# The down projection of a feed-forward layer: seven half-size products in place of eight, with weight sums added by DMAs

## The reference, cut to what matters

```python
h = rms_norm(x, norm_ffn[l])                                         # 512 x 1024
x = x + (jax.nn.silu(h @ w_gate[l]) * (h @ w_up[l])) @ w_down[l]     # (512 x 2816) @ (2816 x 1024)
return x
```

## Time and profile before

| what | us |
|---|---|
| median of three runs | 1574.59 (1573.61 to 1575.96) |
| the profiled execution: span | 1570.6 |
| TensorE busy | 1536.9 (98%) |
| VectorE busy | 1007.2 (64%) |
| ScalarE busy | 832.5 (53%) |
| GpSimd busy | 210.5 (13%) |

### The profile page before, as it was taken

One profiled execution on the slowest core, in us unless ns is written; L12 is line 12 of the kernel. 1 busy time (PEld: TensorE's weight loads), 2 busy tenths in 40 slices (PEclk: granted clock), 3 DMA queues, 4 the chain that ended last, 5 costly groups with the idle time before them and its releaser, 6 DMA issues.

```text
span 1570.6 us, 20022 instructions
## 1 busy us (share of the span) xinstructions
PE 1536.9 (98%) x7872; PEld 1247.3 (79%) x7872; DVE 1007.2 (64%) x1681; ACT 832.5 (53%) x1459; POOL 210.5 (13%) x278
## 2 busy tenths in 40 slices
PE   9999999999999999999989999999999999999999
PEld 8877777788877888888877766888778888888887
DVE  4267977865479998999787786575765333434231
ACT  5278776554456888888863434435434333333220
POOL 1000014522234000000062101111201000000000
PEclk9999999999999999999999999999999999999999
DMA  6122121114547999999943111031212323223232
GB/s 233 65 81 79 56 71 65 54 54 150 214 161 231 375 421 421 421 422 421 326 149 107 54 54 54 28 108 54 81 58 78 108 81 108 92 82 121 67 112 90
DMA packets 78641, 235.89 MB, mean 150 GB/s; under 512 B 6960, under 2 KB 9424, under 8 KB 66256
## 3 DMA queue, kind: packets, MB, share of 16 engines
q1 hardware_dynamic: 68288, 207.62, 36.3%
q10 hardware_dynamic: 6624, 14.88, 2.5%
q0 software_dynamic: 3632, 12.08, 2.0%
HBM read 221.97 MB, written 12.60 MB: 149 GB/s over the span
## 4 chain that ended last, share of the span: by engine, by line
PE 84%; DVE 11%; ACT 2%; issue 1%; DMA 1%; POOL 0%; SPq 0%; DVEq 0%; ACTq 0%; POOLq 0%
PE bank L109 80%; PE bank L112 4%; DVE low L134 2%; DVE REST L124 1%; DVE REST L134 1%; DVE REST L137 1%; ACT REST L115 1%; DVE AL L124 1%; DVE REST L146 1%; DVE REST L143 1%; DVE REST L130 1%; ACT REST L118 1%; ACT CHH L118 0%; DVE R L124 0%; DVE st L140 0%
## 5 line engine op out<-in xcount | busy, mean ns | idle before, releaser
L124 DVE TENSOR_TENSOR low<-slot,CHH 128x1024 fp32r<-128x1024 f32 (+1 forms) x300 | 298.0, 1037 | 117.5 <-ACT CHH L118 116.5
L118 ACT ACTIVATE CHH<-slot 128x1024 fp32r<-128x1024 f32 (+1 forms) x300 | 258.8, 900 | 128.7 <-PE bank L109 56.6
L134 DVE SCALAR_TENSOR_TENSOR low<-slot,smalls,CHH 128x512 fp32r<-128x512 f32 (+1 forms) x232 | 170.3, 766 | 191.2 <-ACT CHH L118 187.3
L109 PE MATMUL bank<-AH,CHH 128*128 128x512 f32 (+1 forms) x640 | 248.5, 388 | 0.2 <-DVE AL L124 0.2
L109 PE MATMUL bank<-AL,CHH 128*128 128x512 f32 (+1 forms) x640 | 242.8, 379 | 0.0
L109 PE MATMUL bank<-AH,low 128*128 128x512 f32 (+1 forms) x640 | 242.6, 379 | 0.0
L118 ACT ACTIVATE CHH<-slot,smalls 128x512 fp32r<-128x512 f32 (+1 forms) x232 | 154.6, 701 | 137.8 <-PE bank L109 68.2
L109 PE MATMUL bank<-CHH,AH 128*128 128x512 f32 x512 | 215.2, 420 | 3.8 <-DVE low L134 2.8
L109 PE MATMUL bank<-low,AH 128*128 128x512 f32 x512 | 200.8, 392 | 0.0
L109 PE MATMUL bank<-CHH,AL 128*128 128x512 f32 x512 | 200.2, 391 | 0.0
L109 PE MATMUL bank<-CHH,XTF 128*128 128x512 f32 x512 | 161.2, 396 | 1.9 <-DVE REST L121 1.1
(11 more groups left out here) (191 smaller groups left out, 2395.4 us busy)
## 6 DMA issues: line engine op xcount, KB each, us to landing
slot<-in_w_in SPq DMA_DIRECT2D x35, 1024.0 KB, 5.1
slot<-in_w_exp_gate SPq DMA_DIRECT2D x32, 1024.0 KB, 13.0
slot<-in_w_exp_up SPq DMA_DIRECT2D x32, 1024.0 KB, 13.2
slot<-in_w_exp_down SPq DMA_DIRECT2D x32, 1024.0 KB, 13.2
slot<-in_w_gate SPq DMA_DIRECT2D x10, 1024.0 KB, 4.9
slot<-in_w_up SPq DMA_DIRECT2D x10, 1024.0 KB, 5.0
slot<-in_w_down SPq DMA_DIRECT2D x10, 1024.0 KB, 5.1
slot<-in_w_out SPq DMA_DIRECT2D x8, 1024.0 KB, 5.1
```

What stands on the lines that cost most here:

```text
L109: return self.e.matmul(out, l, r, start=start, stop=stop) if self.e else Issued()
L118: return self.e.activation(out, in_, ACT.Copy, scale=scale) if self.e else Issued()
L124: return self.e.tensor_tensor(out, a, b, op) if self.e else Issued()
L134: return self.e.scalar_tensor_tensor(out=out, in0=a, scalar=s, in1=b, op0=op0, op1=op1) if self.e else Issued()
```

## The change

Rows of hidden features, tokens and output columns are each halved, and Strassen's scheme in Winograd's form is used: seven products of half size (256 tokens x 1408 features x 512 columns) in place of eight. A product has 11 chunks, and a chunk has 6 matmuls (two token tiles x 3) in place of 12. With A the activations and B the weights, P1 = A11 B11, P2 = A12 B21, P3 = S4 B22, P4 = A22 T4, P5 = S1 T1, P6 = S2 T2, P7 = S3 T3.

- Activations: `up_evac` writes the product into `parts`; GpSimd forms S3 for the first eleven feature blocks and S1, S2, S4 for the others, each 128x256, S2 after S1 and S4 after S2. High parts and low parts of A12, S2, S3, A22, S1 and S4 are made during the down projection, in pieces of up to three blocks (128x768), low parts in place.
- Weights: P1 and P2 load their chunks as before, though splits now take two chunks at once (128x1024; the eleventh chunk alone). P6, P7 and P4 run together over eleven "triples". A triple is one slot with B11, B12, B21 of one feature block, loaded by two DMAs (512 KB and 256 KB), then GpSimd issues a DMA that adds B22 onto B12 in the slot, then VectorE makes two more sums (`weight_sums`), and the three chunks are split at once (128x1536). Triples use five slots, two of them in memory that comes free at the end of `fu20` and of P1. For P5 three slots get B11 (1 MB, 1 MB, 768 KB) and a DMA each that adds B12. P3 loads B22 plainly.
- Order on TensorE: P1, P2, the triples, P5, P3. VectorE's and ScalarE's work is listed unit by unit (a unit `u` is one split: 0 to 5 for P1, 6 to 11 for P2, 12 to 22 the triples, 23 to 28 P5, 29 to 34 P3). P6 and P5 are summed on top of P1 in its banks, after VectorE has added the former sum onto `xr`.

The core of the diff:

```diff
+    def dma_add(self, out, in_):
+        return self.e.dma_start(out, in_, accum_op=ALU.add) if self.e else Issued()
...
-    slot_kb = (0, 8, 16, 48, 144, 152, 160, 136, 176)
+    slot_kb = (0, 8, 16, 48, 144, 152, 160, 136, 176, 94, 104)
...
-    for n in range(2):
-        plan_seg(f"wd{n}", t["w_down_2"][0], 512 * n, 0, nk=FT, part=3)
+    down_rows = t["w_down_2"][0].rearrange("(t k p) n -> p t k n", t=2, p=P)
+    def unit(s, q0, n, at, ready):
+        u = len(units)
+        chunks = range(len(CH), len(CH) + n)
+        for i, c in enumerate(chunks):
+            CH.append((s, q0 + i))
+        cells = range(at, at + n)
+        before = [holds_cell[x] for x in cells if x in holds_cell]
+        holds_cell.update((x, chunks[-1]) for x in cells)
+        units.append((chunks, s.ap[:, q0:q0 + n, :], s.low[:, q0:q0 + n, :],
+                      of[:, a:a + n * 512].rearrange("p (k n) -> p k n", k=n), before, ready))
+    holds_cell = {(D0 - 1 - x) % 8: D0 - 1 - x for x in range(8)}
+    pair_cells = itertools.cycle((0, 2, 4, 6))
+    def plan_block(h, n0, add_row=None):
+        for k in range(0, FK, 4):
+            m = min(4, FK - k)
+            s = plan_slot(next(in_turn), down_rows[:, h, k:k + m, n0:n0 + 512], m, 512, 3)
+            if add_row is not None:
+                s.more = down_rows[:, h, k:k + m, add_row:add_row + 512]
+            for q in range(0, m, 2):
+                unit(s, q, min(2, m - q), next(pair_cells), ("added", s.number) if s.more is not None else None)
+    plan_block(0, 0)
+    plan_block(1, 0)
+    in_turn = itertools.cycle((9, 10, next(in_turn), next(in_turn), next(in_turn)))
+    triples = []
+    for j in range(FK):
+        s = plan_slot(next(in_turn), down_rows[:, 0, j, :].rearrange("p (b n) -> p b n", b=2), 3, 512, 3)
+        s.rest = down_rows[:, 1, j, 0:512]
+        s.more = down_rows[:, 1, j, 512:1024]
+        taken[s.i] += 1
+        s.landed += 16
+        triples.append(s)
+        unit(s, 0, 3, 3 * (j % 2), ("T4", j))
+    pair_cells = itertools.cycle((6, 8, 3, 0))
+    plan_block(0, 0, add_row=512)
+    sums_last = [s for s in slots if s.more is not None][FK:]
+    plan_block(1, 512)
...
+        def product(name, c, part, k, two, first, last):
+            hi, lo = high(c), low(c)
+            pe.wait_ge(*at(("part", part, k if part == A11 else k // 3)))
+            pe.wait_ge(*at(("", "lo", c)))
...
+        sums = pair("P1")
+        for k in range(FK):
+            product("P1", D0 + k, A11, k, sums, k == 0, k == FK - 1)
+        own2 = pair("P2")
+        for k in range(FK):
+            product("P2", D0 + FK + k, A12, k, own2, k == 0, k == FK - 1)
+        own7, own4 = pair("P7"), pair("P4")
+        for i in range(2):
+            pe.wait_ge(*at(("on x", "P1", i, 0)))
+        for k in range(FK):
+            c = D0 + 2 * FK + 3 * k
+            product("P6", c, S2, k, sums, False, k == FK - 1)
+            product("P7", c + 1, S3, k, own7, k == 0, k == FK - 1)
+            product("P4", c + 2, A22, k, own4, k == 0, k == FK - 1)
+        for i in range(2):
+            pe.wait_ge(*at(("on x", "P6", 2 + i, 0)))
+        for k in range(FK):
+            product("P5", D0 + 5 * FK + k, S1, k, sums, False, k == FK - 1)
+        banks.next["main"] += 2
+        own3 = pair("P3")
+        for k in range(FK):
+            product("P3", D0 + 6 * FK + k, S4, k, own3, k == 0, k == FK - 1)
...
+        def unit_high(chunks, raws, lows, highs, before, ready):
+            act.wait_ge(*at(ready) if ready else landed(chunks[0]))
+            for c in before:
+                act.wait_ge(*at(("", "done", c)))
+            act.copy(highs, raws).then_inc(*mark("act_hi", *(("", "hi", c) for c in chunks)))
...
+        def high_of(part, n, *events):
+            for event in events:
+                act.wait_ge(*at(event))
+            act.copy(piece(part_high[part], n), piece(parts[:, part], n), scale=-1.0 if part == S1 else 1.0).then_inc(
+                *mark("act_evac", ("part high", part, n)))
+        gates_done = ("full", "fu20", 1)
...
+            if 15 <= u <= 18:
+                high_of(S1, u - 15, ("", "done", D0 + 2 * FK - 1))
+            if 19 <= u <= 22:
+                high_of(S4, u - 19, ("", "done", D0 + 2 * FK - 1))
...
+        def first_low(k):
+            dve.wait_ge(*at(("S2", k)))
+            dve.wait_ge(*at(("part high", A11, k)))
+            dve.tt(parts_low[:, A11, k, :], parts[:, A11, k, :], part_high[A11][:, k, :].bitcast(F32), ALU.subtract).then_inc(
+                *mark("dve_evac", ("part", A11, k)))
+        def unit_low(chunks, raws, lows, highs, before, ready):
+            for c in chunks:
+                dve.wait_ge(*at(("", "hi", c)))
+            dve.tt(lows, raws, highs.bitcast(F32), ALU.subtract).then_inc(*mark("dve_lo", *(("", "lo", c) for c in chunks)))
         for f0 in range(0, FT, 4):
             def up_evac(j, f0=f0):
                 f = f0 + j
-                s = sgp.buf(("sg", f))
+                of = A11 if f < FK else A12
                 dve.wait_ge(*at(("full", f"fu{f0}", j)))
                 dve.wait_ge(*at(("fgs", f)))
-                dve.tt(s, s, banks.ap((f"fu{f0}", j)), ALU.mult).then_inc(
-                    *mark("dve_evac", ("fum", f), ("free", (f"fu{f0}", j))))
-                dve.wait_ge(*at(("aTh", f)))
-                dve.tt(aT[1][:, f, :], s, aT[0][:, f, :].bitcast(F32), ALU.subtract).then_inc(
-                    *mark("dve_evac", ("aT", f), ("free", ("sg", f))))
+                dve.tt(parts[:, of:of + 2, f % FK, :], *(x.rearrange("p (t n) -> p t n", t=2) for x in (
+                    sgp.buf(("sg", f)), banks.ap((f"fu{f0}", j)))), ALU.mult).then_inc(
+                    *mark("dve_evac", ("a", f), ("free", (f"fu{f0}", j)), ("free", ("sg", f))))
+                if FK + 2 <= f < FT - 1:
+                    first_low(f - FK - 2)
             if f0:
                 drain(seg(f"fg{f0}"))
-            drain(seg(f"fu{f0}", up_evac))
-        for n in range(2):
-            def out_x(i, n=n):
-                xs = xr[:, i, n * 512:(n + 1) * 512]
-                dve.wait_ge(*at(("full", f"wd{n}", i)))
-                dve.wait_ge(*at(("x4", i, n)))
-                dve.tt(xs, banks.ap((f"wd{n}", i)), xs, ALU.add).then_inc(
-                    *mark("dve_evac", ("out", i, n), ("free", (f"wd{n}", i))))
-            drain(seg(f"wd{n}", out_x))
+            for n, _ in enumerate(seg(f"fu{f0}", up_evac)):
+                if f0 == 20 and n in EARLY_UNITS:
+                    unit_low(*units[EARLY_UNITS.index(n)])
+        def low_of(part, n):
+            dve.wait_ge(*at(("part high", part, n)))
+            dve.wait_ge(*at(("S4", FK - 1)))
+            a, b, c = piece(parts_low[:, part], n), piece(parts[:, part], n), piece(part_high[part], n).bitcast(F32)
+            x = dve.stt(a, b, -1.0, c, ALU.mult, ALU.subtract) if part == S1 else dve.tt(a, b, c, ALU.subtract)
+            x.then_inc(*mark("dve_evac", ("part", part, n)))
+        def weight_sums(j):
+            b11, b12, b21 = (triples[j].ap[:, q, :] for q in range(3))
+            dve.wait_ge(*at(("added", triples[j].number)))
+            dve.tt(b11, b12, b11, ALU.add).then_inc(*mark("dve_down", ("T2", j)))
+            dve.wait_ge(*at(("T2", j)))
+            dve.tt(b21, b11, b21, ALU.add).then_inc(*mark("dve_down", ("T4", j)))
+        last_on = {(i, n): ("x4", i, n) for i in range(NT) for n in range(2)}
+        def add_on(name, half, n, bank=None, left=False, done=False):
+            for i in range(2):
+                to = 2 * half + i, n
+                xs = xr[:, to[0], n * 512:(n + 1) * 512]
+                dve.wait_ge(*at(("full", name, i)))
+                dve.wait_ge(*at(last_on[to]))
+                last_on[to] = ("on x", name, *to)
+                events = [last_on[to]]
+                if left:
+                    events.append(("free", (name, i)))
+                if done:
+                    events.append(("out", *to))
+                b = banks.ap((bank or name, i))
+                dve.tt(xs, *((xs, b, ALU.subtract) if n and name != "P3" else (b, xs, ALU.add))).then_inc(*mark("dve_evac", *events))
+        for u, unit in enumerate(units):
+            if 11 <= u < 11 + FK:
+                weight_sums(u - 11)
+            if u >= len(EARLY_UNITS):
+                unit_low(*unit)
+            if u == 1:
+                first_low(FK - 3)
+            if u == 2:
+                first_low(FK - 2)
+                first_low(FK - 1)
+            if 3 <= u <= 4:
+                for n in (2 * u - 6, 2 * u - 5):
+                    low_of(A12, n)
+            if 5 <= u <= 6:
+                for n in (2 * u - 10, 2 * u - 9):
+                    low_of(S2, n)
+            if 7 <= u <= 8:
+                for n in (2 * u - 14, 2 * u - 13):
+                    low_of(S3, n)
+            if u == 9:
+                add_on("P1", 0, 0)
+            if 10 <= u <= 11:
+                for n in (2 * u - 20, 2 * u - 19):
```

(48 more changed lines are left out.)

## The result

The changed kernel takes 1585.64 us (median of four runs, 1584.45 to 1589.07) against 1574.30 for the kernel before: ratio 1.0075, interval 1.0062 to 1.0088. It is 0.75% slower, where 1572.0 was forecast and 1582 was the upper end of the range.

The account below looks back on a forecast made before the run. TensorE alone was taken to bound the down projection. 15.0 us removed, less losses of 5.7 + 2.0 + 4.6 = 12.3, leaves 2.7 gained: 1567.9 profiled, runs 4.0 above, written as 1572.0; range 1565 to 1582.

Parts of the forecast that it names:

- 15.0 us removed: Down projection on TensorE: seven products need 462 matmuls instead of 528, so 66 at 0.2273 us go.
- First loss: From T to the first triple: VectorE's list delays its start to T+35.7 instead of T+30.0, 5.7 us lost.
- T: Zero point of the down projection's times: end of `fu20`, 1447.4 us in the kernel before.
- VectorE's account: VectorE's work before the first triple: free at T+7.2, then 27.7 us of list, plus 0.5 and 0.3, giving T+35.7.
- Second loss: In the triples: how fast a slot comes round through load, addition, sums and split; triples end at T+82.8, 2.0 us lost.
- the rule: Triples' slots: four triples need 4.7 + L + 1.4 + 1.7 + 4.1 us, more than TensorE's 16.4 once L exceeds 4.5.
- L: Time of GpSimd's adding DMA for a triple's slot, taken from gathers: 5.5 us, bounds 4.4 and 8.8.
- Third loss: Way into P5: P6's sum stands behind unit 25, which awaits a 1 MB addition; P5 starts at T+87.4, 4.6 us lost.
- The clock, a rival: Gaps before the first triple and P5 lower TensorE's clock, 18 matmuls costing 4 us more each time: 1576 to 1580; chance 0.10.
- The queues' latency counts, not their rate: Down projection's DMAs: 26 MB in 117 us is 222 GB/s, where 421 was sustained in the experts' stretch.
- The slow rival: Adding DMAs slow, L = 8.8 and 12 us for 1 MB; triples end at T+90.8, kernel at 1579.4; chance 0.18.

Follow-up runs that it names:

- the late pieces: Changed kernel with P3 ahead of P5, plus nine of the S2, S3, A22 pieces split during the triples and P3 instead of before: ratio 1.0021, span 1578.5.

## Why the prediction was wrong, step by step

- **15.0 us removed:** right; where TensorE has no gap it needs 0.229 us a matmul.
- **First loss, 5.7 forecast, 5.9 measured:** the first triple starts at 1483.81 = T+35.9 against T+35.7. VectorE's account held to 0.2 us, the wait of 2.9 us included. That the first triple's own load and addition held it to nearly the same place (T+35.2 with the late pieces) was not in it; only that run showed it.
- **Second loss, 2.0 forecast, 9.6 measured (the triples end at T+90.5).** The way of a slot is what bound the triples: without its additions they need 42.1 us between the low parts, and with six slots and earlier issues 41.2. The terms of the rule (11.9 + L for four triples, 17.4 us by the forecast) were mis-sized: one round of the chain, from 1502.02 to 1522.97, takes 21.0 us. L was put at 5.5 and is 0.3 + 5.0 in the median, but 0.3 + 7.5 in the chain; the load was put at 4.7 and is 0.3 + 5.3 in the median, 0.3 + 5.2 in the chain. So the median of L was forecast well; the round that counted was not the median one. I had taken the additions' own price from a gather, right for one alone, and not asked what they do to the loads beside them: they hold an engine 2.4 times as long as a copy. 1.6 of the 9.6 us is the clock behind the first wait (eight matmuls 0.2 us late each).
- **Third loss, 4.6 forecast, 9.2 measured.** The mechanism and the place were right (unit 25, the second 1 MB addition, the sum P6 behind it). The addition was put at 9.2, which is near what one takes alone (8.9 to 10.5), and took 14.2, beside P5's first addition for 7 us of it (with six slots, issued after the first had landed, it took 11.4); that these DMAs overlap was not in the estimate. Its load was put at 5.1 and took 6.5; the slot came free at T+75.1 instead of T+69.5. The wait is what of this sticks out behind the triples.
- **The clock, a rival with a chance of 0.10:** it came true at both gaps, 1.6 us and 32.3 - 30.0 = 2.3 us, less than its price of 4 us each (its 18 matmuls come from no row; eight were slow behind the first gap). It was no alternative to the other losses but their consequence. The forecast itself had a gap of 4.6 us ahead of P5, and every wait that long lowered the clock in these runs, so that cost belonged in the sum; the one ahead of the first triple, of about 3 us, lowered it in four of the six runs in which it was 2.9 us long.
- **"The queues' latency counts, not their rate":** half right for the triples, whose loss ended without quicker additions once the way of a slot had more room, and wrong for P5, where the engines' share is 1.09 while its additions are in flight together. In the earlier trace rows the down projection takes a share of 0.26 for 90 GB/s, so by this estimate its loads would fill the engines at about 346 GB/s, not 422; its packets are of 2 KB, the experts' of 6.4 KB in the mean (80.93 MB in 12715), which I take for the reason without having tried it. An addition then takes 2.4 times a copy's engine time. The row with the share was in the table and I didn't divide; the 2.4 was in no row.

The slow rival named the right mechanism, with L = 8.8 and 12 us, and gave 1579.4. With the clock's 3.9 us it would be 1583. Its T+90.8 for the end of the triples against T+90.5 is luck in part: L was less than 8.8, the first triple did not wait for its own addition, and the clock added its share. The sum of the measured losses is 5.9 + 9.6 + 9.2 + 2.3 = 27.0, less 15.0: 12.0 of the 12.7 us; T is 0.4 us later and the end behind the last matmul 0.2 us longer.

## What to carry to other kernels

When work moves from a full engine to idle ones, add up the way of one buffer (release, load, addition, sums, split, use) and divide by the buffers, with each DMA at its price beside the others; divide a stretch's GB/s by its DMA share to see roughly what the engines would carry there. A wait of TensorE of 3.3 us or more needs the clock's 1.8 to 3.2 us beside it in the sum; one of 2.1 to 2.9 us cost it here in seven cases of fourteen. A gain can lie in the queue rather than in the data: one addition moved up one unit was worth 5.9 us, and P3 ahead of P5, late pieces, one more slot and earlier loads together made this change faster than the kernel before (0.9944).

## What was not expected of the hardware

An adding DMA held the engines 2.4 times as long as a copy of the same bytes, and plain 256 KB loads beside it landed after 5.3 us instead of 4.1. Two 1 MB additions in flight together took 11.0 and 14.2 us where one alone took 8.9 to 10.5. TensorE's granted clock fell after some idle waits of 2.1 to 2.9 us and not after others of the same length, and the price was not much more after 9.2 us (2.3) than after 2.9 us (1.6).
